# A fused two-block transformer: expert outputs of all passes but the last fetched and weighed by GpSimd during the last pass, the last pass added by TensorE; the even mixer's norm roots in four groups

## The chip, the cores and the metric

The kernel runs on one core of one Trainium2 chip. Times are device microseconds (us) from launch to end. The kernel before takes 3375.63 us, the median of 3 runs (3374.01 to 3377.91). Everything is float32.

## The reference, cut to what matters

256 tokens of width 1024 (and 256 context tokens in the first block) pass two blocks of two layers each. The change touches two places.

Place one, the gated linear attention of layer 0 (4 heads of 128 values, run as two pairs of heads, two directions). Its outputs are normed per token and head, then gated:

```python
def _rms(x, gain, eps=1e-6):
    y = xf * lax.rsqrt(jnp.mean(xf * xf, axis=-1, keepdims=True) + eps)
    return (y * gain.astype(jnp.float32)).astype(x.dtype)
def _gated_readout(o, og, gain):
    return _merge(_rms(o, gain) * jax.nn.silu(og))
```

Place two, the mixture of experts of the very last layer, with the norm and the per-layer input that end the kernel:

```python
def moe_swiglu(x, w_router, w_gate, w_up, w_down):
    top_v, top_i = lax.top_k(logits, TOP_K)             # 2 of 8 experts per token
    top_w = jax.nn.softmax(top_v, axis=-1)
    gates = jnp.sum(jax.nn.one_hot(top_i, N_EXPERTS) * top_w[..., None], axis=-2)
    for e in range(N_EXPERTS):
        out = out + gates[..., e:e + 1] * swiglu(x, w_gate[e], w_up[e], w_down[e])
x = layer_norm(alpha * x + f, ln_ffn_g[i], ln_ffn_b[i])        # alpha * x: "ALPHA X"
x = x + (p[i] @ w_ple_proj[i]) * jax.nn.sigmoid(x @ w_ple_gate[i])
```

## The kernel before, in words

The program is written out by hand, engine by engine, in stages. Between two stages stands `meet()` (L197): each engine drains, raises its semaphore and waits for those of the other three. SyncE issues all weight loads into a ring of three slots (`ring_buf`); it doesn't take part in `meet()`.

**Even mixer, `gla_pairs`.** Sixteen units, eight for each pair of heads (`units`, p = 0 then p = 1), go through a pipeline: TensorE sums and scores, ScalarE exponentials, VectorE masks (L927), GpSimd halves (L894), VectorE adds the levels (`add_levels`, L934), TensorE makes the output (L822, L824), VectorE takes it (`take`, L942). Pair p's token tiles 0 and 1 are complete four units before its end; tile 3 comes with the second last unit and tile 2 with the last. ScalarE squares and sums the outputs (`square`, L859): those of pair 0 while pair 1 runs, all eight of pair 1 after the last unit. GpSimd then takes one root of all 128x16 sums (L904, L906), and VectorE multiplies sixteen 128x128 blocks by root and gate (L970). Then comes a `meet()` and the turning of the result (L256).

**Experts.** `experts` first routes (logits, top two, `place` = the token's rank in its expert, `where` = its row in the DRAM table `moe_rows`, and the number of passes, `total`). A pass handles up to 96 tokens of one expert: 44 MB of weights in twelve items over three slots, an item's load issued when its slot's former item is used up. Seven passes are written out (`FIXED`), the rest run in one hardware loop (L2863) whose count is loaded from `total` by `passes` (L2854); with these inputs the loop runs once, so there are eight passes. In a pass TensorE gathers the tokens of the next one (`gather`, L2919), and the result goes from PSUM through `ye` (ScalarE L3043, VectorE L3083) to `moe_rows` in DRAM (`save`, L2876, in the next pass behind item 2). After the last pass SyncE saves once more, GpSimd fetches each token's two rows with four indirect DMAs (L3103) into the third slot, and VectorE weighs and adds them (L3091, L3093). `clear_rows` (L2647) zeroes the part of `moe_rows` past the first eight passes, much earlier.

**Norm.** `seam_alone` with `LayerNormSeam`: VectorE makes ALPHA X + Y for a token tile (L2436), its statistics (L2439, L2441), GpSimd the root (L2450, L2451), VectorE scales (L2443), TensorE turns (L2483), ScalarE and VectorE write `hT` (L2490, L2498). Behind its roots GpSimd loads the norm's gain and shift (`pool_begin`, L191) and waits for them (L193) before it can reach the `meet()`. `per_layer_input` (L2568, L2576, L2586) ends the kernel; its three weight loads (L223) stand behind the last `save` on SyncE.

## Time and profile before

| what | value |
|---|---|
| median of 3 runs | 3375.63 us |
| profiled execution, its own time | 3372.65 us |
| its span (first to last instruction) | 3370.8 us |
| TensorE busy / VectorE / ScalarE / GpSimd | 3099.1 / 819.7 / 414.5 / 304.9 us |
| granted TensorE clock, mean | 0.96 |
| chain that ended last: TensorE / VectorE / DMA | 81% / 11% / 2% of the span |

1.9 us lie outside the span. All times of the trace count from the span's start. "Idle before" is how long an engine sat before a group of instructions; the arrow names who ended it. The granted clock is 1.00 at 2.4 GHz and 0.50 at 1.2 GHz. TensorE's float32 matmuls appear as two records each, transposes as one.

### The profile page before, as it was taken

The numbers are of one execution on the slowest core, as the hardware profiler recorded it, in microseconds if no ns is written. First come the engines' busy times: TensorE is split into PE (matmuls) and PEld (weight loads), VectorE is DVE, ScalarE is ACT, GpSimd is POOL, SyncE is SP. The second block draws the span as 40 slices with busy tenths as digits, with TensorE's granted clock in tenths as the row PEclk, the third lists the DMA queues.
The fourth block names the chain that finished last, engine by engine and source line by source line (L and its number), as shares of the span: only waits on it lengthen the run. The fifth ranks groups of instructions, "written<-read, shape, count | busy, mean of one in ns | idle before, by whom it ended". The sixth has DMA issues, their size and how long they took to land.

```text
span 3370.8 us, 41515 instructions
## 1 busy us (share of the span) xinstructions
PE 3099.1 (92%) x18118; PEld 1767.8 (52%) x18118; DVE 819.7 (24%) x1556; ACT 414.5 (12%) x1027; POOL 304.9 (9%) x359
## 2 busy tenths in 40 slices
PE   6988779999989999899988999978999999999995
PEld 2456544444447777576656766444434434444442
DVE  1146932000035676500132000253000000000003
ACT  1024121000022212200021000130000000000001
POOL 1123710000002233200000000000000000000000
PEclk9989889999999999999989999978999999999997
DMA  8670001212022122244332343305899999999983
GB/s 345 252 260 1 1 0 63 112 63 106 38 59 63 51 61 60 90 149 167 122 113 113 131 174 138 108 33 204 340 406 359 359 381 388 359 362 407 359 316 117
DMA packets 210612, 609.13 MB, mean 181 GB/s; under 512 B 6076, under 2 KB 55452, under 8 KB 203904
## 3 DMA queue, kind: packets, MB, share of 16 engines
q1 hardware_dynamic: 205024, 592.59, 46.4%
q0 software_dynamic: 4944, 13.28, 1.2%
q8 instruction: 145, 2.38, 0.3%
q10 hardware_dynamic: 464, 0.60, 0.1%
q14 instruction: 35, 0.29, 0.0%
HBM read 600.28 MB, written 6.16 MB: 180 GB/s over the span
## 4 chain that ended last, share of the span: by engine, by line
PE 81%; DVE 11%; issue 3%; ACT 3%; DMA 2%; POOL 1%; POOLq 0%; ACTq 0%; DVEq 0%; PEldq 0%; SPq 0%
PE ps_ffn_gate L606 10%; PE ps_ffn_up L606 10%; PE ps_ffn_down L642 10%; PE ps_moe_down L2971 6%; PE ps_moe_gate L2928 6%; PE ps_moe_up L2928 6%; PE ps_odd L1904 4%; PE ps_lin L1384 3%; PE ps_project L524 3%; PE ps_moe_gate L2933 3%; PE ps_moe_up L2933 3%; PE ps_moe_down L2977 3%; PE ps_lin L296 3%; PE ps_ple_gate L2576 2%; DVE rec_qd L2163 2%
## 5 line engine op out<-in xcount | busy, mean ns | idle before, releaser
L606 PE MATMUL ps_ffn_gate<-hT,ring_buf 128*128 128x256 f32 (+1 forms) x1152 | 341.5, 450 | 4.4 <-issue 2.4
L606 PE MATMUL ps_ffn_up<-hT,ring_buf 128*128 128x256 f32 (+1 forms) x1152 | 336.7, 445 | 1.3
L642 PE MATMUL ps_ffn_down<-ring_buf,ffn_hiddenT 128*128 128x512 f32 x752 | 325.9, 593 | 3.0 <-issue 3.0
L606 PEld LDWEIGHTS ps_ffn_gate<-hT,ring_buf 128*128 128x128 f32 x1152 | 221.1, 193 | 119.3 <-issue 98.1
L606 PEld LDWEIGHTS ps_ffn_up<-hT,ring_buf 128*128 128x128 f32 x1152 | 218.0, 190 | 110.2 <-issue 90.0
L1904 PE MATMUL ps_odd<-ring_buf,hT 128*128 128x256 f32 (+2 forms) x1024 | 237.0, 386 | 8.1 <-ACT hg_kT L2039 6.4
L642 PEld LDWEIGHTS ps_ffn_down<-ring_buf,ffn_hiddenT 128*128 128x128 f32 x752 | 141.8, 190 | 181.9 <-issue 181.9
L691 DVE TENSOR_TENSOR ffn_hiddenT<-ffn_silu_buf,ps_ffn_up 128x256 f32<-128x256 f32 (+1 forms) x72 | 36.2, 502 | 725.4 <-PE ps_ffn_up L606 725.3
L3070 DVE TENSOR_TENSOR moe_hidden_buf<-moe_silu_buf,ps_moe_up 128x768 f32<-128x768 f32 (+1 forms) x32 | 27.3, 854 | 748.4 <-PE ps_moe_up L2933 748.4
L1904 PEld LDWEIGHTS ps_odd<-ring_buf,hT 128*128 128x128 f32 x1024 | 174.4, 193 | 55.4 <-ACT hg_kT L2039 7.9
L2928 PE MATMUL ps_moe_up<-ring_buf,moe_xg_buf 128*64 128x512 f32 (+1 forms) x1024 | 199.5, 542 | 0.0
L2971 PE MATMUL ps_moe_down<-ring_buf,moe_hiddenT 128*64 128x512 f32 x768 | 170.1, 595 | 0.0
L2928 PE MATMUL ps_moe_gate<-moe_third,moe_xg_buf 128*64 128x512 f32 (+1 forms) x768 | 142.8, 524 | 0.0
L663 ACT ACTIVATE ffn_silu_buf<-ps_ffn_gate 128x256 f32<-128x256 f32 (+1 forms) x72 | 32.3, 449 | 840.5 <-PE ps_ffn_gate L606 840.5
L1384 PE MATMUL ps_lin<-ring_buf,hT 128*128 128x448 f32 (+1 forms) x384 | 132.4, 498 | 0.0
L2928 PEld LDWEIGHTS ps_moe_up<-ring_buf,moe_xg_buf 128*64 128x64 f32 x1024 | 70.6, 137 | 111.5 <-issue 103.3
L3019 ACT ACTIVATE moe_silu_buf<-ps_moe_gate 128x768 f32<-128x768 f32 (+1 forms) x32 | 23.4, 730 | 697.1 <-PE ps_moe_gate L2933 697.1
L2971 PEld LDWEIGHTS ps_moe_down<-ring_buf,moe_hiddenT 128*64 128x64 f32 x768 | 53.0, 137 | 103.3 <-issue 102.5
L1384 PEld LDWEIGHTS ps_lin<-ring_buf,hT 128*128 128x128 f32 x384 | 71.6, 192 | 62.6 <-issue 58.2
L2933 PE MATMUL ps_moe_up<-ring_buf,moe_xg_buf 128*32 128x256 f32 (+1 forms) x2048 | 103.5, 354 | 0.0
L2928 PEld LDWEIGHTS ps_moe_gate<-moe_third,moe_xg_buf 128*64 128x64 f32 x768 | 53.0, 137 | 81.9 <-issue 73.8
L3103 POOL DMA_INDIRECT moe_third<-moe_rows,moe_where x4 | 4.0, 988 | 988.0 <-DMA moe_rows<-moe_ye 987.1
(491 smaller groups left out, 3498.0 us busy)
## 6 DMA issues: line engine op xcount, KB each, us to landing
ring_buf<-in_w_exp_up_dram SPq DMA_DIRECT2D x24, 4096.0 KB, 16.3
ring_buf<-in_w_exp_down_dram SPq DMA_DIRECT2D x24, 4096.0 KB, 16.0
moe_third<-in_w_exp_gate_dram SPq DMA_DIRECT2D x16, 4096.0 KB, 17.6
mod_pieces<-in_mod_w_dram SPq DMA_DIRECT2D x40, 1024.0 KB, 6.4
ring_buf<-in_w_exp_gate_dram SPq DMA_DIRECT2D x8, 4096.0 KB, 17.6
ring_buf<-in_odd_w_in_dram SPq DMA_DIRECT2D x40, 512.0 KB, 5.3
moe_third<-in_w_exp_gate_dram SPq DMA_DIRECT2D x8, 2048.0 KB, 10.8
ring_buf<-in_w_exp_up_dram SPq DMA_DIRECT2D x8, 2048.0 KB, 7.8
```

What stands on the lines that cost most here:

```text
L296: mm = nc.tensor.matmul(ps[n % 4][:, 0:hi - lo], hT[:, k, t * P:(t + 1) * P], view[:, k, o:o + hi - lo], start=k == 0, stop=k == parts - 1)
L524: mm = nc.tensor.matmul(ps_y[i % 2][:, h * 512:(h + 1) * 512], of(k, t), view[:, k, :], start=k == 0, stop=k == KD - 1)
L606: mm = nc.tensor.matmul(ps[:, 0:wide], view[:, k, i * P:(i + 1) * P], hT[:, k, first_col:first_col + wide], start=k == 0, stop=k == KD - 1)
L642: mm = nc.tensor.matmul(ps_y[i % 2][:, h, :], hidT[:, b, i * P:(i + 1) * P], view[:, b, h * 512:(h + 1) * 512], start=first, stop=end)
L1384: mm = nc.tensor.matmul(ps_lin[:, n % 4, 0:hi - lo], hT[:, k, t * P:(t + 1) * P], view[:, k, o:o + hi - lo], start=k == 0, stop=k == KD - 1)
L1904: mm = nc.tensor.matmul(ps[:, 0:width], hT[:, k, t * P:(t + 1) * P], view[:, k, 0:width], start=k == 0, stop=k == KD - 1)
L2163: last = nc.vector.tensor_tensor(in_blocks(qd[:, d, l - 1, :], x), in_blocks(qd[:, d, l, :], x), query_factors(d, x), ALU.mult)
L2576: mm = nc.tensor.matmul(ps_gate[i][:, cols], hT[:, k, t * P:(t + 1) * P], view[:, k, :], start=k == 0, stop=k == KD - 1)
L2928: nc.tensor.matmul(ps[j * 64:(j + 1) * 64, 0:half], xg[:, k, 0:WIDE], w[:, k, j * half:(j + 1) * half], start=k == 0, stop=k == KD - 1, ti ...
L2933: mm = nc.tensor.matmul(ps[j * 32:(j + 1) * 32, half:half + quarter], xg[:, k, WIDE:ROOM], w[:, k, j * quarter:(j + 1) * quarter], start=k ...
L2971: nc.tensor.matmul(ps_y[j * 64:(j + 1) * 64, 0:512], x, w[:, b, j * 512:(j + 1) * 512], start=c == 0 and b == 0, stop=c == NP - 1 and b == ...
L2977: mm = nc.tensor.matmul(ps_y[j * 32:(j + 1) * 32, 512:768], x, w[:, b, j * 256:(j + 1) * 256], start=c == 0 and b == 0, stop=c == NP - 1 a ...
```

## The change

**Even mixer.** The squares of pair 1 are taken in three groups: tiles 0 and 1 after unit 11, tile 3 after unit 14, tile 2 after unit 15. GpSimd takes four roots: pair 0 and the first half of pair 1 between the halves of units 14 and 15, the other two after them. VectorE gates in four places: four blocks before the last `add_levels`, eight behind it, two and two after the last `take`.

**Experts.** GpSimd fetches during the last pass: it waits until all passes but the last are saved, fetches the four sets of rows into the ring's third part (free then), makes ALPHA X in `Y`, and adds the rows times `early`, the routing weight where the row comes from an earlier pass and 0 where it comes from the last. The last pass is not saved. Instead VectorE makes `pick_g` (the pick matrix times the gate) at the start of the loop's pass, TensorE turns it (two transposes behind the dummy `gather`), ScalarE copies it to `back`, and after the loop TensorE multiplies it with `ye` (`scatter`: four 96x128 by 96x512 float32 matmuls) into two PSUM tensors, which VectorE adds to `Y` into X. New small operations on VectorE during routing make `gates` (ahead of the table of passes) and `early` (behind it).

**Norm.** X arrives summed, so L2436 falls away; gain and shift are loaded by GpSimd at the start of the experts stage into `Y[:, 0:2]`. `clear_rows` writes one more block. `START` (the first value of each semaphore) is 16, so that the new waits against registers stay positive.

```diff
-START = 4
+START = 16
...
+                square(1, (0, 1), n - 4)
+                square(1, (3,), n - 1)
+                square(1, (2,), n)
...
+                    if u == n - 2:
+                        root(1, 0, 4, slice(0, 2))
+                        root(2, 0, 2, slice(2, 4))
+                root(3, 3, 4, slice(2, 4))
+                root(4, 2, 3, slice(2, 4))
...
+                    if u == n - 1:
+                        gated(0, (0, 1), 1)
                     add_levels(u)
+                gated(0, (2, 3), 1)
+                gated(1, (0, 1), 2)
                 take(n - 1)
...
+                gated(1, (3,), 3)
+                link_v(gated(1, (2,), 4))
...
+            if not self.summed:
+                link_v(nc.vector.scalar_tensor_tensor(out=x, in0=x, scalar=ALPHA, in1=self.made(i), op0=ALU.mult,
+                                                      op1=ALU.add))
...
                 seam.pool_steps(pool)
-                seam.pool_begin(pool)
...
-                                 for p in range(EXPERTS, 13)))
+                                 for p in range(EXPERTS - 1, 13)))
...
+                for i in range(2):
+                    link_v(nc.vector.tensor_scalar(gates[:, i, :, 0], one[:, i, 0, :], w01[:, i, 0:1], None, ALU.mult))
+                    link_v(nc.vector.scalar_tensor_tensor(out=gates[:, i, :, 0], in0=one[:, i, 1, :],
+                                                          scalar=w01[:, i, 1:2], in1=gates[:, i, :, 0],
+                                                          op0=ALU.mult, op1=ALU.add))
+                for h in range(1, PARTS):
+                    last = nc.vector.tensor_copy(gates[:, :, :, h], gates[:, :, :, 0])
...
-                save(n_passes - 1).then_inc(S["moe_all_saved"].handle, 16)
+                sp.wait_ge(S["moe_weighed"].handle, S["moe_weighed"].at(2))
...
+                def scatter(n):
+
+                    pe.wait_ge(S["moe_ye_a"].handle, S["moe_ye_a"].at(0) + n)
+                    pe.wait_ge(S["moe_ye_v"].handle, S["moe_ye_v"].at(0) + n)
+                    pe.wait_ge(S["moe_back"].handle, S["moe_back"].at(0) - FIXED + n)
+                    for i, ps in enumerate((ps_y[:, :], ps_t[:, :, :].rearrange("p k n -> p (k n)"))):
+                        for h in range(2):
+                            mm = nc.tensor.matmul(ps[:, h * 512:(h + 1) * 512], back[:, i, :],
+                                                  ye[:, h * 512:(h + 1) * 512], start=True, stop=True)
+                        mm.then_inc(S["moe_scatter"].handle, 1)
...
+                            if not isinstance(p, int):
+                                turned_back(p)
                         down(p, n0, c)
...
-                for i in range(2):
-                    dve.wait_ge(moe_fetched[2 * i], 16)
...
+                for i, ps in enumerate((ps_y[:, :], ps_t[:, :, :].rearrange("p k n -> p (k n)"))):
+                    dve.wait_ge(S["moe_weighed"].handle, S["moe_weighed"].at(i + 1))
+                    dve.wait_ge(S["moe_scatter"].handle, S["moe_scatter"].at(i + 1))
+                    nc.vector.tensor_tensor(X[:, 2 + i, :], Y[:, 2 + i, :], ps, ALU.add)
...
+                seam.pool_begin(pool)
+                n_passes = passes(pool)
+                pool.wait_ge(S["moe_saved"].handle, S["moe_saved"].at(0) - 16 + n_passes * 16)
+                pool.sem_inc(S["moe_earlier_saved"].handle, 1)
                 pool.wait_ge(S["moe_places"].handle, S["moe_places"].at(1))
...
+                for i in range(2):
+                    link_g(nc.gpsimd.tensor_scalar(Y[:, 2 + i, :], X[:, 2 + i, :], ALPHA, None, ALU.mult))
+                pool.wait_ge(moe_fetched, 64)
+                for i in range(2):
+                    for c in range(2):
+                        row = fetched[:, 2 * i + c, :]
+                        link_g(nc.gpsimd.tensor_scalar(row, row, early[:, i, c:c + 1], None, ALU.mult))
+                        last = nc.gpsimd.tensor_tensor(Y[:, 2 + i, :], Y[:, 2 + i, :], row, ALU.add)
```

VectorE at the end of the even mixer, before (L934 is `add_levels`, L942 `take`, L970 the gating):

```order
L927 TENSOR_TENSOR ring_buf<-ps_pair_scores,pair_mask_table 128x1024 x2
L942 TENSOR_TENSOR even_A<-even_A,ps_pair_out 128x256
L934 TENSOR_REDUCE hT<-ring_buf 128x256
L942 TENSOR_TENSOR even_A<-even_A,ps_pair_out 128x256
L970 SCALAR_TENSOR_TENSOR even_A<-even_A,pair_rstd_buf 128x128 x16
```

and after the change (the same operations are L936, L951, L943, L969):

```order
L936 TENSOR_TENSOR ring_buf<-ps_pair_scores,pair_mask_table 128x1024 x2
L951 TENSOR_TENSOR even_A<-even_A,ps_pair_out 128x256
L969 SCALAR_TENSOR_TENSOR even_A<-even_A,pair_rstd_buf 128x128 x4
L943 TENSOR_REDUCE hT<-ring_buf 128x256
L969 SCALAR_TENSOR_TENSOR even_A<-even_A,pair_rstd_buf 128x128 x8
L951 TENSOR_TENSOR even_A<-even_A,ps_pair_out 128x256
L969 SCALAR_TENSOR_TENSOR even_A<-even_A,pair_rstd_buf 128x128 x4
```

Twelve of the sixteen gatings moved ahead of the last `take`. VectorE from the end of the last pass to the first scaling of the norm, before (L3083 writes `ye`, L2863 ends the loop, L3091 and L3093 weigh):

```order
L3083 COPY moe_ye<-ps_moe_down 32x256 x4
L2863 REGISTER_ALU
L2863 COMPARE_AND_BRANCH
L3091 TENSOR_SCALAR Y<-moe_third,moe_w 128x1024
L3093 SCALAR_TENSOR_TENSOR Y<-moe_third,moe_w,Y 128x1024
L3091 TENSOR_SCALAR Y<-moe_third,moe_w 128x1024
L3093 SCALAR_TENSOR_TENSOR Y<-moe_third,moe_w,Y 128x1024
L210 UNCONDITIONAL_BRANCH
L2529 UNCONDITIONAL_BRANCH
L2436 SCALAR_TENSOR_TENSOR X<-X,Y 128x1024
L2439 BN_STATS ln_stats<-X 128x6 x2
```

and after (L3171 adds the scattered rows):

```order
L3162 COPY moe_ye<-ps_moe_down 32x256 x4
L2905 REGISTER_ALU
L2905 COMPARE_AND_BRANCH
L3171 TENSOR_TENSOR X<-Y,ps_moe_down 128x1024
L3171 TENSOR_TENSOR X<-Y,ps_moe_turn 128x1024
L210 UNCONDITIONAL_BRANCH
L2551 UNCONDITIONAL_BRANCH
L2462 BN_STATS ln_stats<-X 128x6 x2
```

Four weighings and the ALPHA sum gave way to two additions. TensorE behind the loop, after the change (L3021 is the last of the down projection, L3043 `scatter`, L2506 the norm's turning; before, nothing stood between the branch and the turning):

```order
L3021 MATMUL ps_moe_down<-moe_third,moe_hiddenT 32x256 x16
L2905 REGISTER_ALU
L2905 COMPARE_AND_BRANCH
L3038 REGISTER_ALU
L3040 REGISTER_ALU
L3043 MATMUL ps_moe_down<-moe_ye,moe_back_buf 128x512 x2
L3043 MATMUL ps_moe_turn<-moe_ye,moe_back_buf 128x512 x2
L210 UNCONDITIONAL_BRANCH
L2541 UNCONDITIONAL_BRANCH
L2506 MATMUL ps_turned_4<-const,Y 128x128 x16
```

So TensorE's new work stands directly behind its loop branch, with two register operations ahead of it.

## Rows read from the trace of the kernel before

**Rows 1.** Chain of waits, last 80 us: start us, us, what.

```profile
3290.92 1.91 PE ps_moe_down L2977 x32
3294.26 0.44 DVE moe_ye L3083
...
3294.93 3.66 DMA moe_rows<-moe_ye
...
3303.39 9.69 DMA moe_third<-moe_rows,moe_where
...
3314.91 1.24 DVE X L2436
...
3324.05 4.92 DMA ln_shift<-in_ln_ffn_b_dram
...
3329.66 1.11 PE ps_ple_proj L2568 x4
```

**Rows 2.** Timeline of the norm: start us, us, engine, line, operation.

```profile
3316.17 1.29 DVE L2439 BATCH_NORM_STATS2 ln_stats<-X 128x6 f32<-128x512 f32 x2
...
3326.00 1.50 ACT L2490 ACTIVATE hT<-ps_turned,ln_columns 128x128 f32<-128x128 f32 x4 [2.96 <-PE ps_turned L2483]
```

**Rows 3.** Timeline of TensorE in the per-layer input.

```profile
3340.20 7.03 PE L2576 MATMUL ps_ple_gate<-ring_buf,hT 128*128 128x512 f32 x16
```

**Rows 4.** Stretches after the last pass: busy by engine, clock, DMA share, GB/s.

```profile
3293.00:3296.00 3.00, 0.00 (x0) 0.00 (x0) 1.64 (x4) 1.18 (x2) 0.00 (x0) 0.86 0.09 27
3296.00:3330.00 34.00, 4.29 (x18) 3.49 (x19) 13.79 (x22) 3.01 (x8) 6.98 (x10) 0.50 0.71 256
```

**Rows 5.** The loop line's TensorE branch: ns min/median/max, first and last start.

```profile
L2863 PEldq COMPARE_BRANCH  x1: 114/114/114, 3291.4 to 3291.4; - x1
```

**Rows 6.** The drain line of meet(), from 3285 to 3331 us.

```profile
L204 PEldq DRAIN  x2: 13/1008/2002, 3294.8 to 3324.0; - x2
```

**Rows 7.** DMA issued at 3184.23 us: size, us to landing.

```profile
ring_buf<-in_w_exp_up_dram SPq DMA_DIRECT2D x1, 4096.0 KB, 18.1
```

**Rows 8.** Timeline of TensorE: the first use of that item.

```profile
3206.07 7.09 PE L2928 MATMUL ps_moe_up<-ring_buf,moe_xg_buf 128*64 128x512 f32 x32
```

**Rows 9.** DMA queues, 3304 to 3308 us: packets, MB, share of 16 engines.

```profile
q0 software_dynamic: 267, 1.02, 64.2%
q1 hardware_dynamic: 290, 0.59, 39.5%
```

**Rows 10.** Timeline of the end of the even mixer.

```profile
429.40 2.48 POOL L894 TENSOR_TENSOR ring_buf<-ring_buf 128x512 f32<-128x512 f32 x2 [3.92 <-DVE ring_buf L927]
...
431.92 1.89 DVE L934 TENSOR_REDUCE hT<-ring_buf 128x256 f32<-128x1024 f32 x1 [1.14 <-POOL ring_buf L894]
...
435.98 0.42 DVE L942 TENSOR_TENSOR even_A<-even_A,ps_pair_out 128x256 f32<-128x256 f32 x1 [2.17 <-PE ps_pair_out L824]
436.43 0.31 ACT L859 ACTIVATE pair_junk<-even_A 128x128 f32<-128x128 f32 x1 [29.03 <-DVE even_A L942]
...
440.29 2.93 POOL L906 TENSOR_TENSOR pair_rstd_buf<-pair_rstd_buf,const 128x16 f32<-128x16 f32 x1
443.25 4.29 DVE L970 SCALAR_TENSOR_TENSOR even_A<-even_A,pair_rstd_buf 128x128 f32<-128x128 f32 x16 [6.86 <-POOL pair_rstd_buf L906]
448.11 1.57 PEld L256 LDWEIGHTS ps_turn<-const,even_A 128*128 128x128 f32 x8 [12.47 <-issue]
```

**Rows 11.** Groups of GpSimd by form: busy us, mean ns.

```profile
L1489 POOL TENSOR_TENSOR qk_rstd_buf<-qk_rstd_buf,const 128x10 f32<-128x10 f32 x4 | 8.7, 2178 | 0.3
L1839 POOL TENSOR_TENSOR hg_rstd<-hg_rstd,const 128x2 f32<-128x2 f32 x8 | 6.9, 864 | 0.7
```

**Rows 12.** The line of passes(), around 2335 us.

```profile
L2854 PEldq TENSOR_LOAD <-moe_total x1: 491/491/491, 2336.8 to 2336.8; - x1
```

**Rows 13.** The line of gate()'s wait, around 2335 us.

```profile
L2942 PEldq EVENT_SEMAPHORE  x1: 51/51/51, 2338.4 to 2338.4; - x1
```

**Rows 14.** Timeline of VectorE while it routes.

```profile
2327.39 1.03 DVE L2786 TENSOR_SCALAR moe_one<-const,moe_idf 128x8 f32<-128x8 f32 x4
```

More of the change, by code:

```diff
@@ L852, in decays, with square @@
                         .then_inc(S["rec_decays"].handle, 1)
-                def square(p):
-                    act.wait_ge(S["rec_state"].handle, S["rec_state"].at((p + 1) * per))
-                    for t in range(4):
+                def square(p, tiles, taken):
+                    act.wait_ge(S["rec_state"].handle, S["rec_state"].at(taken))
+                    for t in tiles:
                         for e in range(2):
@@ L952, in take, with gated @@
                     last.then_inc(S["rec_state"].handle, 1)
+                def gated(p, tiles, roots):
+                    dve.wait_ge(S["rec_rms"].handle, S["rec_rms"].at(roots))
+                    for t in tiles:
+                        for e in range(2):
+                            h = 2 * p + e
+                            gate = A[:, t, O_G + h * GV:O_G + (h + 1) * GV]
+                            last = nc.vector.scalar_tensor_tensor(out=gate, in0=made(p, t)[:, e, :],
+                                                                  scalar=rstd[:, t, h:h + 1], in1=gate,
+                                                                  op0=ALU.mult, op1=ALU.mult)
+                    return last
                 link_v(nc.vector.memset(state[:, :, :, :], 0.0))
@@ L2388, in program, with __init__ @@
     class LayerNormSeam:
-        def __init__(self, cx, layer, site, tiles, kept, deferred=False):
+        def __init__(self, cx, layer, site, tiles, kept, deferred=False, summed=False,
+                     rows=None):
             self.layer, self.site, self.tiles, self.kept, self.deferred = layer, site, tiles, kept, deferred
-            self.gain = sb(cx, "ln_gain", [P, D])
-            self.shift = sb(cx, "ln_shift", [P, D])
+            self.summed = summed
+            self.gain = sb(cx, "ln_gain", [P, D]) if rows is None else rows[:, 0, :]
+            self.shift = sb(cx, "ln_shift", [P, D]) if rows is None else rows[:, 1, :]
             self.stats = sb(cx, "ln_stats", [P, 2, 2, 6])
@@ L2708, in experts @@
             chosen = sb(cx, "moe_chosen_buf", [P, 2, EXPERTS])
+            gates = sb(cx, "moe_gates", [P, 2, EXPERTS, PARTS])
+            early = sb(cx, "moe_early", [P, 2, 2])
+            limit = sb(cx, "moe_limit", [P, 1])
+            pick_g = sb(cx, "moe_pick_g_buf", [P, 2, ROOM])
+            back = sb(cx, "moe_back_buf", [ROOM, 2, P])
             slot = sb(cx, "moe_slot", [P, 2, 2, EXPERTS])
@@ L3003, in _ @@
                 other_passes(pe, n_passes, one_pass)
+                scatter(n_passes)
             @block.scalar
```

92 lines of the change are left out of this document (55 added, 37 removed).

## The prediction

> **What bounds the kernel now.** I read the page first: TensorE is busy 92% of the span and carries 81% of the chain that ended last. So a change off TensorE pays only where TensorE stands still, and there are two such places in reach. Then I read the chain of waits at the end [rows 1]: the last pass ends at 3292.8 us, and TensorE's next weights-bound work starts at 3329.66. In between stand the copy to `ye`, the save's landing, four fetches (9.69 us from the last issue to landing), weighing, the norm, and last the landing of `ln_shift` (4.92 us), which holds GpSimd and with it the meeting of the engines. The reader is to see that nearly all of it is DMA and VectorE. Third, the timeline at the end of the even mixer [rows 10]: the last output is taken at 435.98, TensorE turns the result at 448.11, and between lie squares, one root of 2.93 us and sixteen gatings of 4.29 us, one behind the other. In the passes themselves TensorE has no idle stretch worth naming, and there the DMAs are close behind it [rows 7, 8].
>
> **Even mixer: -8.1 us.** Before, from the end of `take` (435.98 + 0.42 = 436.40) eight squares and a scaling pass until the root starts at 440.29, 3.86 us; the root takes 2.93 and the gating 4.29, which ends at 447.54; 0.57 us later TensorE starts [rows 10]. After: two squares (an eighth of about 3.45 us each, 0.9), hand-over and scaling 0.4, a root of two sums 0.86 [rows 11], two gatings at 4.29/16 = 0.27 each with their start, 0.6, and the same 0.57. From about 436.5 this gives 439.9 against 448.11, 8.2 us less; I take 8.1. What hides the rest: the roots of eight and of four sums stand on GpSimd ahead of its last halves, where it sat idle 3.92 us [rows 10]. Between 864 ns for two sums and 2178 ns for ten [rows 11] a sum costs 0.164 us, so the two roots cost 1.85 and 1.19, with two scalings 3.7 us in all: it fits by 0.2. Four gatings (1.07 us) fit into VectorE's idle 1.14 before `add_levels`, and eight (2.15) into the 2.17 before the last `take` [rows 10]. All three fits are tight; what they overrun goes on the path in full, since halves, levels and output of the last unit wait there. If scalings on slices cost twice as much and every cover fails a little, 1.5 us come back: bounds -6.5 and -8.6. The next stage finds its weights in the ring, so nothing there takes the gain back.
>
> **End of the passes: -17.1 us.** `ye` is ready at 3294.70 [rows 1] and the norm's first statistics start at 3316.17 [rows 2]: 21.5 us. In its place comes `scatter`. Its earliest start: TensorE's loop branch runs at 3291.4 [rows 5], while its next instruction, the drain, came at 3294.8 [rows 6], with the matmuls over at 3292.8. I read these 3.3 us as the time to get the code behind the loop. It ends just when `ye` is ready, so `scatter` starts at 3294.9. The Trainium skill ("Runtime: NRT & Kernel Launch", Instruction fetch mechanics) says that a branch whose target isn't in the loaded window stalls for a fetch by DMA; by that rule the cost is right, and the trace agrees with 3.3 us on TensorE.
>
> A float32 matmul of 512 columns takes 7.03/8 = 0.88 us at the full clock [rows 3], four take 3.5, and 7.0 at half of it. The granted clock is 0.86 between 3293 and 3296 and 0.50 behind [rows 4]: it fell soon after 3295, when TensorE had stood still for some 2.3 us. With new work from 3294.9 it may stay up, fall at once, or fall and come back; I take the middle, 5.2 us, so the products are there at 3300.1. VectorE's addition of the first tile hides beside the second product, the second costs 1.24 (as L2436, which also reads two tiles [rows 1]), the meeting 0.5: statistics at 3301.9, that is 14.3 us earlier. Ends: 15.9 (full clock) and 12.5 (half throughout). The second L2436 goes as well, on the path of the second tile: 1.2. The last write to `hT` ends at 3326.00 + 1.50 = 3327.5 [rows 2]; with 0.5 for the meeting TensorE could have started at 3328.0 and not at 3329.66 [rows 1], since GpSimd was waiting for `ln_shift`. That load now stands in front: 1.6. Together 14.3 + 1.2 + 1.6 = 17.1. What is late next: the weights of the per-layer input. SyncE issues them now once the slots are free and GpSimd has weighed, so they are no later than before, and before they were issued behind the save. They land in front of TensorE.
>
> GpSimd's new work must end before 3294. Two scalings for ALPHA X, four more, four additions on 128x1024: by L894 (2.48 us for two of 512 columns, rows 10) at most 2.5 us each, 25 us, from about 3197 on, behind the fetches. It ends near 3232, 60 us early.
>
> **What it costs in the passes: +2.1 us.** (a) The fetch moves 4 x 512 KB beside the weights of the last pass. Two queues share: 1.02 MB and 0.59 MB in 4 us, the fetch's queue had 64% [rows 9]; at 0.40 MB/us the 2.1 MB take 5.2 us of all engines. The item issued at 3184.23 lands 18.1 us later, at 3202.3 [rows 7], and TensorE begins on it at 3206.07 [rows 8]: 3.8 us to spare. If the fetch comes wholly ahead of it, it is 1.4 us late, and what follows is delayed no further, since each later item then has that stall in hand. I take +1.4; the ends are 0 and 5.2. The Trainium skill ("DMA: Bandwidth & Descriptors", Queues, rings and completion order) has each engine take turns between its queues packet by packet. That speaks against the change: a fetch of less urgent rows isn't queued behind the weights. The trace agrees, with more than half for the fetch's queue. (b) Two transposes and register operations in the loop: +0.3. (c) Routing: the six operations for `gates` come ahead of the table for which TensorE waits in `passes`. Its load starts at 2336.8 [rows 12] and with the register operations behind it takes some 0.9 us, while `gate` waits until 2338.4 anyway [rows 13]: 0.7 to spare. Four small operations take 1.03 us [rows 14] or less, two copies 0.2: late by 0.4. Ends 0 and 0.6. `early` comes behind the table, the sixth zero block and GpSimd's loads at the front beside other work: nothing, for GpSimd has nothing else to do in the passes, and the first items have many us to spare. `START` is free.
>
> **Sum.** -8.1 - 17.1 + 1.4 + 0.3 + 0.4 = -23.1 us. From the profiled execution's 3372.65 (span 3370.8 and 1.9 around it) that gives 3349.5. The median shown is 3375.63, 3.0 above the profiled one; on it the sum gives 3352.5, which I predict.
>
> **Rivals.**
> 1. The clock holds up during `scatter` and the fetch finds the DMAs free: 15.9 in place of 14.3, no stall. -8.1 - 18.7 + 0.7 = -26.1, 3349.5. For it: TensorE stands still for only 2.1 us. Against: the clock fell after 2.3 us [rows 4], and the queues are full [rows 9].
> 2. The way out costs twice. `scatter` sits between the loop and the next branch, to the meeting. If TensorE must fetch again for that one, 3.3 us come on the path, where before they lay beside the save. The time is worked out from rows 5 and 6; the Trainium skill's rule on branches (same page and section as above) would have it so. With 1.5 us more from the tight covers of the even mixer or the stall: -23.1 + 4.8 = -18.3, 3357.3. For it: the one branch out of this loop did cost this. Against: TensorE reaches the branch while its matmuls still run, so most may hide.
> 3. Slower than before: the fetch starves the weight stream. Place: the items of the last pass behind 3197. Price: all that it delays them beyond 3.8 us. It decides from 3.8 + 24.5 = 28 us of delay; at 33 us the kernel takes 3380. Against: even with 64% of the engines the fetch is through after 5.2/0.64 = 8 us [rows 9], and no row shows rows of 4 KB running so much slower.
> 4. The change doesn't do what it says, because GpSimd is late: it would need 60 us more work than 25. I give it nothing of its own and count it with 3.
>
> **How the numbers follow.** Forecast 0.57, rival 1 0.20, rival 2 0.20, rivals 3 and 4 0.03. A difference under 0.2% (6.7 us) is no change for this measurement. All cases but the last are faster by 18 us or more: faster 0.95, same 0.02 (some of 2 with both ends of its costs), slower 0.03. The forecast's own range is 3349 to 3356 by the bounds of the clock (1.6 and 1.8) and of the stall. For 8 in 10 I go from 3346 (rival 1, even mixer at its best, runs 2 us lower as the three shown differ) to 3361 (rival 2 with 3.7 us more stall).
>
> **What would show it.** Right: TensorE turns the even mixer's result 3.9 us behind `take` in place of 12.1; the products start within 0.3 us of `ye`; the statistics start 7.2 us behind it; no wait on `ln_shift`; one stall of about 1.4 us on a weight item between 3200 and 3220. Wrong: halves of the last unit starting later than GpSimd's neighbours allow, a gap between the branch and the drain behind `scatter`, several stalls on weights, or additions on VectorE waiting for GpSimd.

## The result and the profile after

| | before | after |
|---|---|---|
| median of the runs, us | 3375.76 (3374.01 to 3377.91, 4 runs) | 3354.65 (3353.03 to 3357.11, 4 runs) |
| profiled execution: time, span | 3372.65, 3370.8 | 3353.03, 3351.2 |
| granted clock of TensorE, mean | 0.960 | 0.963 |

The ratio is 0.9935, 95% interval 0.9922 to 0.9947. The change takes 21.1 us off the median, with 18 to 26 by the interval. Forecast were 23.1 us and 3352.5. (The median of before has moved by 0.13 us because a fourth run has joined the three of the first table.)

The timeline of the changed kernel at the end of the passes answers to [rows 1, 2] (start us, length us, engine, line, operation, in brackets the idle time before it and what ended it):

```profile
3292.95 0.86 DVE L3162 COPY moe_ye<-ps_moe_down 32x256 f32<-32x256 f32 x2
3294.05 1.98 PE L3043 MATMUL ps_moe_down<-moe_ye,moe_back_buf 96*128 96x512 f32 x4 [2.13 <-DVE moe_ye L3162]
...
3295.87 1.88 PE L3043 MATMUL ps_moe_turn<-moe_ye,moe_back_buf 96*128 96x512 f32 x4
...
3297.86 1.22 DVE L3171 TENSOR_TENSOR X<-Y,ps_moe_turn 128x1024 f32<-128x1024 f32 x1 [0.49 <-PE ps_moe_turn L3043]
3299.50 1.29 DVE L2462 BATCH_NORM_STATS2 ln_stats<-X 128x6 f32<-128x512 f32 x2 [0.42 <-issue]
...
3309.89 1.12 PE L2590 MATMUL ps_ple_proj<-const,ple_in 128*128 128x128 f32 x4 [1.84 <-ACTq L204]
```

`ye` is complete at 3293.82. The products start 0.23 us later, the statistics 5.7 us later, and TensorE goes on with the per-layer input 16.1 us later; before it was 21.5 and 35.0. No wait on `ln_shift` is left. The stretches of the changed kernel (busy us by engine, clock, DMA share, GB/s) answer to [rows 4]: the clock is whole up to 3299 and then at half for 14 us, where before it was at half for 37.

```profile
3290.00:3299.00 9.00, 5.62 (x42) 2.36 (x40) 4.05 (x6) 1.19 (x2) 0.00 (x0) 1.00 1.05 393
3299.00:3313.00 14.00, 7.05 (x23) 5.06 (x24) 10.19 (x20) 4.89 (x10) 1.50 (x4) 0.52 0.10 40
```

The end of the even mixer after the change answers to [rows 10]:

```profile
430.09 2.49 POOL L896 TENSOR_TENSOR ring_buf<-ring_buf 128x512 f32<-128x512 f32 x2 [0.50 <-DVE ring_buf L936]
431.06 0.41 DVE L951 TENSOR_TENSOR even_A<-even_A,ps_pair_out 128x256 f32<-128x256 f32 x1
431.38 2.15 DVE L969 SCALAR_TENSOR_TENSOR even_A<-even_A,pair_rstd_buf 128x128 f32<-128x128 f32 x4
432.94 0.70 POOL L906 TENSOR_TENSOR pair_rstd_buf<-pair_rstd_buf,const 128x2 f32<-128x2 f32 x1
433.46 1.87 DVE L943 TENSOR_REDUCE hT<-ring_buf 128x256 f32<-128x1024 f32 x1
...
437.50 0.42 DVE L951 TENSOR_TENSOR even_A<-even_A,ps_pair_out 128x256 f32<-128x256 f32 x1
...
439.20 0.70 POOL L906 TENSOR_TENSOR pair_rstd_buf<-pair_rstd_buf,const 128x2 f32<-128x2 f32 x1
439.93 0.61 DVE L969 SCALAR_TENSOR_TENSOR even_A<-even_A,pair_rstd_buf 128x128 f32<-128x128 f32 x2 [1.49 <-POOL pair_rstd_buf L906]
441.12 3.77 PE L256 MATMUL ps_turn<-const,even_A 128*128 128x128 f32 x16 [3.66 <-POOLq L204]
```

TensorE turns the result 3.6 us behind the start of `take`, against 12.1. And the waits of TensorE in the last pass (waited for: us in total, times, longest):

```profile
PE ps_moe_down L3015 <- ACT moe_hiddenT L3089: 1.3, 2, 0.7
PE ps_moe_down L3015 <- DMA ring_buf<-in_w_exp_down_dram: 0.8, 1, 0.8
PE ps_moe_up L2970 <- DMA ring_buf<-in_w_exp_up_dram: 0.2, 1, 0.2
```

**Where the time went.** I cut the execution at seven starts that all the kernels have: the mixer's first L798, the turning L256 behind it, the 21st projection matmul behind that, the odd mixer's first matmul, the first expert matmul, the end of the last `ye`, the first matmul of the per-layer input's projection. Each number is the difference of two such times in one profile. Four rows (e1, e2, e5, e12) are experiments told below.

| us | to mixer | to turning | to 21st proj. | to odd | to expert | to `ye` | to per-layer | to the end |
|---|---|---|---|---|---|---|---|---|
| before | 302.4 | 145.70 | 17.00 | 535.16 | 1338.23 | 956.18 | 34.97 | 41.2 |
| before, further profile (e12) | 302.7 | 147.59 | 18.70 | 536.55 | 1339.48 | 956.18 | 35.03 | 41.3 |
| experts' part alone (e2) | 301.7 | 145.73 | 17.00 | 535.16 | 1338.90 | 959.55 | 16.07 | 41.8 |
| mixer's part alone (e1) | 303.9 | 137.85 | 18.97 | 536.67 | 1339.63 | 956.15 | 35.00 | 41.3 |
| after | 303.1 | 138.05 | 18.72 | 536.57 | 1339.79 | 957.61 | 16.07 | 41.3 |
| after, further profile (e5) | 301.1 | 143.85 | 18.98 | 536.70 | 1340.03 | 957.44 | 16.07 | 41.4 |

Read against the first profile of before, the change won 7.65 in the mixer and 18.9 at the end, paid 1.43 in the passes, and seems to have lost 1.7 + 1.4 + 1.6 in three stretches between mixer and experts, and 0.7 ahead of the mixer: 19.6 us of span in all. These three losses are what the experiments had to explain first. (e2's 959.55 holds a further 1.7 us at half clock: 0.72 was granted between 2337 and 2343, where the changed kernel had 1.00.)

### The profile page after: what moved, and what is told of

Its sections match the earlier page's. It is cut to its first block, busy times and chain, and to the rows that moved or that the text cites. A ratio compares the mean times of both kernels' runs of the same rounds, so it can differ in the third digit from the quotient of the medians.

```text
span 3351.2 us, 41580 instructions
## 1 busy us (share of the span) xinstructions
PE 3108.1 (93%) x18128; PEld 1771.5 (53%) x18128; DVE 819.6 (24%) x1564; ACT 414.9 (12%) x1028; POOL 333.8 (10%) x376
## 4 chain that ended last, share of the span: by engine, by line
PE 80%; DVE 10%; issue 3%; ACT 3%; DMA 2%; another core or an unknown queue 1%; POOL 1%; POOLq 0%; ACTq 0%; DVEq 0%; PEldq 0%
PE ps_ffn_gate L606 10%; PE ps_ffn_up L606 10%; PE ps_ffn_down L642 10%; PE ps_moe_down L3015 6%; PE ps_moe_gate L2970 5%; PE ps_moe_up L2970 5%; PE ps_odd L1924 4%; PE ps_lin L1404 4%; PE ps_project L524 3%; PE ps_moe_down L3021 3%; PE ps_moe_up L2975 3%; PE ps_moe_gate L2975 3%; PE ps_lin L296 3%; PE ps_ple_gate L2598 2%; DVE rec_qd L2183 2%
## 5 line engine op out<-in xcount | busy, mean ns | idle before, releaser
L3147 DVE TENSOR_TENSOR moe_hidden_buf<-moe_silu_buf,ps_moe_up 128x768 f32<-128x768 f32 (+1 forms) x32 | 27.3, 855 | 747.1 <-PE ps_moe_up L2975 726.5
```

## The experiments

My theory after the result (A): two parts of the forecast held or came out better, but a part of the mixer's gain is given back behind it by TensorE's clock. In the changed kernel the clock is at half from 432.3 to 452.8 although TensorE is back at 441.12, so L351 runs at half clock; before it ran at the full one. Rival (B): these stretches fall otherwise in every execution, and the whole gain arrives.

**e1, the mixer's part alone; e2, the experts' part alone.** e1 is the kernel before with the hunks of `square`, `root` and `gated`; e2 is the kernel after without them:

```diff
-                        square(0, range(4), per)
-                square(1, (0, 1), n - 4)
-                square(1, (3,), n - 1)
-                square(1, (2,), n)
+                        square(0)
+                square(1)
```

> The kernel before with the even mixer's four groups alone; the experts' end, the norm rows and the gates as before. Theory A (about 3 us of what the mixer wins is given back behind it, because TensorE restarts 7 to 8 us earlier into a stretch at half clock that ends no earlier, and what is left arrives at the end): the turning L256 starts 7 to 8 us earlier than in the kernel before, the routing 3 to 5 us earlier, and the time is 3371 to 3373, a gain of 3 to 5 us. Rival B (the low stretches fall by chance from run to run, and the whole gain arrives): 3367.5 to 3369, a gain of 7 to 8 us. If the gated half came out at nothing by the clock as well, 3374 or more.

> The change without the even mixer's part: fetches, ALPHA X, weighed rows and adds on GpSimd beside the last pass, norm rows in front, gates early. Theory A: the end of the passes gives 18 to 20 us (19.8 less 1.1 of stall, with the routing's +0.4): 3356 to 3358 us. Rival B (the end gives only what the prediction took, 17.1, less 1.4 and 0.7): 3360 to 3361 us. Between this kernel and the whole change lies what the even mixer is really worth: 2 to 4 us by A, 7 to 8 us by B.

Measured: e1 ratio 0.9976 (0.9966 to 0.9986), that is -8.1 us (-4.7 to -11.5); median 3370.93 against 3379.03 for the kernel before, measured beside it. e2 0.9954 (0.9941 to 0.9967), -15.5 us (-11 to -20). Together 23.6, the whole change's 21.9 (by its ratio) within the intervals: the parts add up. e1's gain is what B said, and e2's lies nearer to B's 15.0 (17.1 less 1.4 and 0.7) than to A's 18; but both intervals still reach A's numbers (5 and 18), and the median of e2, 3362.29, lies above what either had named, as the kernel before was 3.3 us slower beside it than beside the change. L351 took 3.8 us in e1, as A had it, and 2.0 in e2. The times leaned to B and the profiles to A.

**e12, the kernel before once more,** unedited, for a further profile.

> The kernel before, unedited, for a further profile. Theory A expects L351 at 2.0 us and the 21st projection matmul 17.0 us behind the turning, as in the first profile and in that of the experts' part alone; 34.9 to 35.1 us from the last ye to L2568's restart; 535.2 us from the 21st projection matmul to the odd mixer and 1338 to 1339 from there to the first expert matmul, where kernels with an early turning had 536.6 to 536.8 in six of seven and 1339.6 to 1340.1. If these last two differ by chance alone, one of them stands at the later kernels' number here.

Its timeline, time 3379.31 us:

```profile
435.98 1.22 PE L822 MATMUL ps_pair_out<-ring_buf,hT 128*128 128x256 f32 x2 [5.03 <-DVE hT L934]
436.99 1.06 PE L824 MATMUL ps_pair_out<-even_A,hT 128*128 128x128 f32 x4
450.27 3.77 PE L256 MATMUL ps_turn<-const,even_A 128*128 128x128 f32 x16 [12.22 <-POOLq L204]
454.96 2.93 PE L351 MATMUL ps_turned<-mod_lines,const 2*128 2x512 f32 x6 [0.93 <-ACTq L204]
```

The unchanged kernel also shows L351 at half clock (3.78 us for its eight, six in this window), and all three "losses" of the table: 18.70, 536.55, 1339.48. They need no change to appear, and the first profile of before was a lucky one. (Of the third, 1.6 us, e12 shows 1.25; the routing, below, has the rest.) The reverse holds too: e7 and e10 (below), which turn early, have the short times in the last two stretches (535.08 and 1338.85, 535.09 and 1338.41), though e7 then has 959.44 in the passes, as e2. So A falls as an account of the second and third loss: they come with where the stretches at half clock happen to lie.

What stays open is the first one, the 1.7 us behind the turning. L351 took 3.8 us in all eight profiles that have an early turning and idle time before it, and in one of the three with the late turning (before, e2, e12). In ten of these eleven the stretch at half clock around the mixer's end is 20.4 to 20.5 us long (27.3 in e12). In before and e2 it was over 1.0 us ahead of L351, which started 21.4 and 21.5 us behind its beginning; in the eight with the early turning L351 started 12.6 to 13.6 us behind it and so lay inside. So this loss looks like more than chance. The times can't tell: e1's interval of 7 us has room for 1.7. Four pairs of profiles can be made of before and e12 with the changed kernel and e5; their spans differ by 19.6, 15.3, 26.2 and 21.9 us. One pair tells a difference no better than that, and the repeated runs are needed for the rest.

**e3, rows fetched later in the last pass.**

```diff
                 pool.wait_ge(S["moe_saved"].handle, S["moe_saved"].at(0) - 16 + n_passes * 16)
+                pool.wait_ge(S["moe_gate"].handle, S["moe_gate"].at(3) - NP + n_passes * NP)
                 pool.sem_inc(S["moe_earlier_saved"].handle, 1)
```

> The whole change, but GpSimd fetches the rows only when the fourth of the last pass's gate products... is through, some 17 us later, when the weight queues have run ahead of TensorE. Theory: the two waits of the last pass on weights (0.24 and 0.83 us, together 1.07) come from the fetches' bytes beside the weight items and are gone; GpSimd is done with the adds at about 3245 instead of 3229, still 29 us before the two transposes need them. Time 1.0 us under the whole change, 3353 to 3354. Rival: the weight stream is short there whoever else moves bytes (the wait stands in the kernel before as well, elsewhere), then the stall stays and the time is the same; a second rival is that the four fetches only move the wait to a later item, same time.

Measured: ratio 0.9929 (0.9917 to 0.9941), 3353.09 us. TensorE's waits in the last pass were then

```profile
PE ps_moe_down L3015 <- ACT moe_hiddenT L3089: 1.3, 2, 0.7
```

and nothing on a DMA. From the first expert matmul to `ye` it took 956.41 (956.40 in e10, which has the same edit), against 957.61 in the changed kernel and 956.18 before. So the stall is the fetch's doing, worth 1.2 us, and can be had back by waiting. GpSimd started the fetch 55.9 us before `ye` was complete, where it was 103.0 in the changed kernel: 47 us later and not the 17 that I had expected. Its last addition still ended 19.7 us ahead of `ye`. In the time the 1.2 us can't be told from the change's own.

**e4, the norm's rows behind the passes again.**

```diff
                 seam.pool_steps(pool)
+                seam.pool_begin(pool)
...
-                seam.pool_begin(pool)
                 n_passes = passes(pool)
```

> The whole change, but the norm's two rows (ln_gain, ln_shift) are issued by GpSimd behind the passes again, when it enters the norm. Theory: the second tile's ScalarE step waits for ln_shift, as it did in the kernel before at 3316.17 to 3326.00; since the statistics now start 5.7 us behind the rows instead of 12, and GpSimd reaches its issues no earlier than the meeting ahead of the norm, the rows land 6 to 7 us after the issue and the first tile waits too: +2 to +4 us, 3357 to 3359. The prediction's own term for the rows' landing was 1.6 us. Rival: the landing hides behind the statistics and roots of 5 us, under +0.5 us.

Measured: ratio 0.9944 (0.9931 to 0.9957), 3358.59 us, 5.5 above e3 measured beside it. Its timeline:

```profile
3295.08 3.55 PE L3044 MATMUL ps_moe_turn<-moe_ye,moe_back_buf 96*128 96x512 f32 x4
...
3300.38 1.29 DVE L2462 BATCH_NORM_STATS2 ln_stats<-X 128x6 f32<-128x512 f32 x2 [0.43 <-issue]
...
3306.01 1.01 POOL L191 DMA_DIRECT2D Y<-in_ln_ffn_g_dram  x1
3307.02 0.56 POOL L191 DMA_DIRECT2D Y<-in_ln_ffn_b_dram  x1
...
3312.61 1.11 PE L2591 MATMUL ps_ple_proj<-const,ple_in 128*128 128x128 f32 x4 [3.69 <-POOLq L204]
```

TensorE went on 19.62 us behind `ye` in place of 16.07. Two things lie in the 3.55. The second product fell into half clock (3.55 us against 1.88) and put the statistics at 7.39 us instead of 5.69: 1.70, chance again. The rest, 1.85, is TensorE waiting longer for GpSimd (3.69 us against 1.84 for the meeting), which issued the rows only behind its roots. e6 and e9 below, with statistics as late as here (7.38) and the rows in front, went on 17.77 us behind `ye`, 1.85 earlier than e4. That bears out the forecast's 1.6 for the norm rows. My +2 to +4 covers the median but not for its reason: the first tile didn't wait, and the rows alone cost less than 2.

**e5, the change once more,** unedited, beside e6 to e8.

> The whole change once more, unedited, on the chip and in the call of the next three. If the ratio of the first measurement (0.9935) is a property of the kernel, it comes again within 0.0015. If the stretches at half clock fall where they will from execution to execution, the profile shows them elsewhere: theory A says that the one behind the even mixer begins at 431 to 434 and ends at 452 to 456 again, and that L351 takes about 3.8 us in it; rival B says that its place is chance, and L351 then takes 2.0 us as before in about half the profiles.

Measured: 0.9928 (0.9914 to 0.9942), 3353.57 us: the result repeats. Its mixer took 5.8 us longer than in the first profile (143.85 against 138.05) at a mean granted clock of 0.83 against 0.88 over it, while the stretch from `ye` to the per-layer input was the same to 0.01 us. L351 took 3.8 us, where B let me expect 2.0 in half the profiles: this is the part of A that stays open.

**e6 and e9, TensorE kept at work at the mixer's end.** Nothing reads these products. e6:

```diff
+                def keep(count):
+                    for _ in range(count):
+                        nc.tensor.matmul(bank_rest[:, P:512], ident, const[:, P:512], start=True, stop=True)
+                keep(14)
                 output(n - 1)
+                keep(10)
```

> The whole change, and TensorE multiplies const into an unused part of a PSUM bank while it waits at the end of the even mixer: 14 matmuls of 384 columns ahead of the last unit's output, 10 behind it, about 0.32 us each at full clock. Nothing reads them. Theory A (what the mixer won is partly given back because TensorE restarts inside the stretch at half clock): the clock stays at its upper level over the turning L256, L351 and the first matmuls of the projection L524; L351 falls from 3.8 to 2.0 us, the first eight L524 from 5.6 to 3.4, the turning from 3.8 to 3.4: 3.5 to 4.5 us under the unedited change. Rival B (the clock falls there whatever TensorE does, or the time comes back at a later stretch): the same time or, if the 24 matmuls hold back the last unit or the turning, up to 4 us more.

e9 has `keep(8)` and `keep(5)`.

> As the kernel of e6, but 8 matmuls of 384 columns ahead of the last unit's output and 5 behind it. In e6 each ran as two instructions of 0.33 us, so that 14 and 10 of them took 9.2 and 6.6 us and held the output back by 4.0 us and the turning by 2.2 more; these take 5.3 and 3.3 us and fit into the idle 5.5 and 3.7. Theory A: the turning starts as in the unedited change and the first 21 projection matmuls are through 15.9 us behind it (e6) instead of 18.7 to 19.2; before the change it was 17.0: 3 us less in the profile, and 1 to 4 us in the time. Rival B: the clock falls all the same in the 0.2 to 0.5 us that stay idle, and the 18.7 to 19.2 stay.

e6 measured 0.9936 (0.9923 to 0.995), e9 0.9926 (0.9912 to 0.9939), 3352.59 us. The timeline of e9:

```profile
432.91 5.33 PE L844 MATMUL ps_pair_rest<-const 128*128 128x384 f32 x16
438.57 0.70 PE L822 MATMUL ps_pair_out<-ring_buf,hT 128*128 128x256 f32 x2 [0.33 <-DVE hT L949]
439.10 0.61 PE L824 MATMUL ps_pair_out<-even_A,hT 128*128 128x128 f32 x4
439.55 3.39 PE L844 MATMUL ps_pair_rest<-const 128*128 128x384 f32 x10
444.15 1.09 PE L256 MATMUL ps_turn<-const,even_A 128*128 128x128 f32 x8 [1.21 <-POOLq L204]
...
447.56 2.23 PE L351 MATMUL ps_turned<-mod_lines,const 2*128 2x512 f32 x8 [0.93 <-ACTq L204]
```

The clock held over the turning in both; in e6 over L351 too (1.99 us), while in e9 it fell inside L351, for 3.4 us. From the turning to the 21st projection matmul it took 15.67 us (e6 15.86) against 18.6 to 19.2 in the kernels with an early turning and idle there. Locally 3 us are won, as expected. In e6 each matmul became two instructions of 0.33 us, twice what I had reckoned; by the profile they held the last output back by 3.3 us and the turning by 3.2 more, and the median was 3357.01, 3.4 above e5's. In e9 they fit into the idle time, but its time differs from e5's by 1 us in 3353, less than the runs can tell.

**e7, the same around the norm.** `ps_g` and `spare` aren't read.

```diff
                         mm.then_inc(S["moe_scatter"].handle, 1)
+                    nc.tensor.matmul(ps_g[:, 0:512], ident, const[:, 0:512], start=True, stop=True)
...
+                keep(3)
                 for i in range(len(tiles)):
                     seam.pe_turn(pe, i)
+                    keep(2)
```

> The whole change, and TensorE multiplies const into PSUM that nobody reads around the norm behind the passes: 1 matmul of 512 columns behind the scatter, 3 ahead of the first turning, 2 behind each turning. Theory: the 13.7 us at half clock from 3299.5 are gone or shorter; what stands in them of TensorE's on the path is the rest of the two turnings (about 0.4 us) and the head of L2598 (8.2 against 7.0 us in the kernel before): 1.5 to 2.3 us under the unedited change. Rival: the gaps left, up to 2 us, are enough for the clock to fall, then the same time or, by the matmuls in TensorE's way at half clock, up to 1 us more.

Measured: 0.9926 (0.9912 to 0.9939), 3352.11 us. The stretch that stood at 0.52 is now whole:

```profile
3299.00:3313.00 14.00, 11.73 (x42) 5.62 (x41) 10.87 (x20) 4.90 (x10) 1.50 (x4) 1.00 0.17 69
```

From `ye` to the end of the 16th L2598 record it took 23.05 us, against 25.18 to 25.75 in the six kernels whose products also ran at full clock: some 2.2 won (2.1 to 2.7), as expected by its stretch; the time, 1.5 us under e5's, can't tell it.

**e8, four gatings moved from before `add_levels` to the end.**

```diff
-                    if u == n - 1:
-                        gated(0, (0, 1), 1)
                     add_levels(u)
...
                 gated(1, (3,), 3)
+                gated(0, (0, 1), 1)
                 link_v(gated(1, (2,), 4))
```

> The whole change, but the four gatings that stood ahead of the last unit's add_levels (L969 at 431.38, 2.15 us for four, where two later ones take 0.61) stand in VectorE's last idle stretch, the 1.48 us ahead of the last gating. Theory: they were slow because GpSimd's L896 ran beside them, held up add_levels by 1.1 to 2.1 us, and now cost nothing, or 0.6 us at most: add_levels starts 1 us earlier or more and the turning L256 starts 0.9 us earlier. In the time that is 0.9 us less if it all arrives. Rival: VectorE is held by L896 itself at that place (add_levels waits for the halves of GpSimd), so it starts when it did and the four gatings now add up to 1 us at the end.

Measured: 0.9935 (0.9921 to 0.9948), 3355.46 us. Its timeline:

```profile
429.95 0.41 DVE L951 TENSOR_TENSOR even_A<-even_A,ps_pair_out 128x256 f32<-128x256 f32 x1
431.50 1.89 DVE L943 TENSOR_REDUCE hT<-ring_buf 128x256 f32<-128x1024 f32 x1 [1.14 <-POOL ring_buf L896]
...
435.89 1.66 DVE L969 SCALAR_TENSOR_TENSOR even_A<-even_A,pair_rstd_buf 128x128 f32<-128x128 f32 x6
438.15 0.62 DVE L969 SCALAR_TENSOR_TENSOR even_A<-even_A,pair_rstd_buf 128x128 f32<-128x128 f32 x2 [0.60 <-POOL pair_rstd_buf L906]
...
439.35 3.77 PE L256 MATMUL ps_turn<-const,even_A 128*128 128x128 f32 x16 [3.83 <-POOLq L204]
```

`add_levels` (L943) starts 1.55 us behind `take` instead of 2.40, waiting 1.14 for GpSimd as it did before the change. The six later gatings come one every 0.28 us, and the last two wait for GpSimd's root, as in the changed kernel. From the start of the second last `take` to the turning it took 9.4 us, against 10.05 to 10.10 in the seven profiles that have the change's mixer unedited: 0.7 of the 0.9 expected, clear of the scatter of that stretch, and unseen in the time (1.9 above e5's median, within the scatter of the runs).

**e11, the gates behind the table.**

```diff
-                for i in range(2):
-                    link_v(nc.vector.tensor_scalar(gates[:, i, :, 0], one[:, i, 0, :], w01[:, i, 0:1], None, ALU.mult))
...
                 nc.vector.sem_inc(S["moe_table"].handle, 1)
+                for i in range(2):
+                    link_v(nc.vector.tensor_scalar(gates[:, i, :, 0], one[:, i, 0, :], w01[:, i, 0:1], None, ALU.mult))
...
```

> The change with the gates' six instructions on VectorE behind the experts' table instead of ahead of it. Theory: VectorE's chain to the table is 1.2 us shorter, and TensorE's first expert matmul no longer waits for the table: it starts 6.9 to 7.1 us behind the first L2961 instead of 7.4. In the time 0.3 to 0.5 us, which the rounds cannot tell from nothing. Rival: the wait was for the rows copied by ScalarE, and the 7.4 stay.

Measured: 0.9930 (0.9917 to 0.9944), 3353.64 us. The first expert matmul starts 7.04 us behind the first L2961 in place of 7.41 to 7.42 (nine profiles); before the change 6.86 and 7.04. The theory holds: 0.4 us in this stretch.

**e10, all of these together** (e3, e7, e8, e11, `keep(6)` and `keep(5)` in the mixer).

> The change with all that helped by its own stretch of the profile: rows fetched late (e3), TensorE kept at work around the norm (e7) and at the even mixer's end (6 matmuls ahead of the last output and 5 behind it), four gatings last (e8), gates behind the table (e11). If the stretches add up: 1.2 + 2.1 + 3 + 0.8 + 0.3 = 7.4 us under the unedited change, 3346 to 3348. Rival: what is won early meets a later stretch at half clock and up to 3 us of it are given back, 3349 to 3351.

Measured: 0.9912 (0.9897 to 0.9927), 3349.95 us, the lowest of all, 2.2 to 3.7 under e7, e9, e11 and e5; but its interval overlaps theirs, so that it beats the changed kernel isn't shown. I had expected 3346 to 3348; it is the rival's 3349 to 3351 that came. Its timeline shows where a part of the 7.4 is missing:

```profile
443.66 1.09 PE L256 MATMUL ps_turn<-const,even_A 128*128 128x128 f32 x8 [1.65 <-POOLq L204]
...
447.54 3.78 PE L351 MATMUL ps_turned<-mod_lines,const 2*128 2x512 f32 x8 [0.93 <-ACTq L204]
...
3292.27 3.77 PE L3055 MATMUL ps_moe_down<-moe_ye,moe_back_buf 96*128 96x512 f32 x4 [2.13 <-DVE moe_ye L3175]
3295.84 3.46 PE L3055 MATMUL ps_moe_turn<-moe_ye,moe_back_buf 96*128 96x512 f32 x4
```

In this execution the clock fell behind the mixer in spite of the added matmuls, and both products ran at half clock: the statistics started 9.02 us behind `ye`, 3.3 more than in e7.

## Why the prediction was right, step by step

- **Even mixer, -8.1.** Right. To the turning -7.65 in the profile, -8.1 (-4.7 to -11.5) by e1. The whole stage varies by more than that between executions (138.05 and 143.85), but the stretch that was changed doesn't: from the start of the second last `take` to the turning it took 17.74 to 17.78 us in the three profiles with the old mixer and 10.05 to 10.10 in the seven with the new one, 7.7 less. The pieces moved against each other. The tail behind `take` came out 0.3 better. The covers did fail by 0.85, within the 1.5 that the text had allowed: `add_levels` starts 2.40 us behind that `take` (431.06 to 433.46), and 1.55 before the change, by this line of before and the 431.92 of [rows 10]:

```profile
430.37 0.41 DVE L942 TENSOR_TENSOR even_A<-even_A,ps_pair_out 128x256 f32<-128x256 f32 x1
```

  The four gatings between them took 2.15 us instead of 1.07. The line's own view of that stretch, and then that of e8 (operation, count, duration in ns as least/median/most, first and last start):

```profile
L969 DVE SCALAR_TENSOR_TENSOR even_A<-even_A,pair_rstd_buf x4: 339/351/1341, 431.4 to 433.2; 128x128 f32<-128x128 f32 x4
```

```profile
L969 DVE SCALAR_TENSOR_TENSOR even_A<-even_A,pair_rstd_buf x16: 342/344/354, 433.3 to 438.4; 128x128 f32<-128x128 f32 x16
```

  The first of them took 1.34 us while GpSimd's L896 ran to 432.58 beside it (1.34 to 1.36 in all nine profiles with a gating there); in e8, where none stands beside L896, all sixteen take 0.34 to 0.35. The Trainium skill ("SBUF — State Buffer", SBUF: two separate sides) says that a VectorE operation with two SBUF inputs and a GpSimd operation that reads SBUF lock each other out, whichever starts first, for the whole instruction; the traces of the change and of e8 agree for L896. They don't show it for the small roots: beside L906 at 432.94 two gatings took 0.34 and 0.36 us, and the root its 0.70, as long as the one at 439.20 with nothing beside it. GpSimd's roots took 1.67 and 1.01 us where I had taken 1.85 and 1.19, and fitted.
- **End of the passes, -17.1.** The mechanism was right and the term too small: TensorE went on 18.9 us earlier behind `ye`. The mis-sized piece is `scatter`: I took 5.2 us, a middle between full and half clock, and it took 3.7. That is rival 1's clock (its free DMAs didn't come). Over the ten other profiles with `scatter` the statistics stood 5.7 us behind `ye` in six, 7.4 in three and 9.0 in one, 6.5 in the mean, so my 7.2 was no bad price but a little dear. The norm rows were worth 1.85 by e4 (I had 1.6).
- **The code behind the loop.** The row on which I built 3.3 us, TensorE's drain at 3294.8 [rows 6], doesn't carry it: in the changed kernel TensorE was past its branch and at `scatter`'s first instruction 0.2 us later, and then waited for `ye`.

```profile
L2905 PEldq COMPARE_BRANCH  x1: 110/110/110, 3290.6 to 3290.6; - x1
L3038 PEldq ALU_OP  x1: 36/36/36, 3290.7 to 3290.7; - x1
L204 PEldq DRAIN  x1: 3722/3722/3722, 3294.1 to 3294.1; - x1
```

  The last start is the drain behind `scatter`, issued beside its matmuls and over when they are. So the path pays nothing for code, neither on leaving the loop nor at the drain, and rival 2 is out as a price. That no fetch took place isn't shown: one of up to 3.1 us would lie hidden in the wait for `ye` (the next instruction ran at 3293.9). By the Trainium skill's rule on branches ("Runtime: NRT & Kernel Launch", Instruction fetch mechanics) a stall was due only for code outside the loaded window; this trace has no visible one. What fills the 3.3 us in the kernel before stays open: no wait stands there in the program, and the drain came 0.14 us behind the end of `ye` in all three profiles that have it so (before, e12, e1). The start of the products came out right because `ye` was as late as the supposed fetch, which is luck.
- **The fetch, +1.4, and transposes, +0.3.** Measured: two stalls, 0.24 and 0.83, and 1.43 in all from the first expert matmul to `ye`, where 1.7 were forecast. e3 shows that 1.2 of it is the fetch. The size was right, the form was not: I had one stall of 1.4 us and nothing behind it, and the larger of the two (0.83) came on the next item. The queues took nearly equal shares, and not the 64% for the fetch of [rows 9]; this is the changed kernel from 3197 to 3204 us (packets, MB, share of 16 engines):

```profile
q1 hardware_dynamic: 376, 1.47, 52.8%
q0 software_dynamic: 383, 1.37, 49.1%
```

  Rival 3 needed 28 us of delay. The item issued at 3181.93 landed 22.1 us later, 4 more than in [rows 7]:

```profile
ring_buf<-in_w_exp_up_dram SPq DMA_DIRECT2D x1, 4096.0 KB, 22.1
```

  GpSimd's last addition ended at 3229.3, forecast near 3232, with some luck: it began 6 us earlier than the 3197 of the forecast and then waited 6.65 us for the rows, and its scalings took 2.85 us, above my bound of 2.5.
- **Routing, +0.4.** Right: +0.38 to +0.56 in the profiles, and e11 takes 0.4 back.
- **The ranges.** The range of its own, 3349 to 3356, is narrower at its upper end than its terms give: 1.8 for the clock and 3.8 for the stall on 3352.5 make 3358.1. The measured 3354.65 lies inside either. (The squares' 3.86 us are 3.89 from 436.40 to 440.29, which changes nothing.)
- **What the sum left out:** the scatter between executions. The stretches at half clock move between profiles of one kernel, and one of them moved costs or gives 1.3 to 1.9 us. The sum -23.1 stands within the four pairs of profiles (-15.3 to -26.2) and within the interval of the runs (-18 to -26). The four terms as the first pair of profiles has them add up to -7.65 - 18.9 + 1.43 + 0.4 = -24.7; 1.5 of the 1.6 beyond the forecast is the clock in `scatter`, which was good in that profile. That the forecast came within some 2 us of the measured median says no more than that it lies inside this scatter.

## What to carry to other kernels

Before you explain a loss found by comparing two profiles, take the unchanged kernel's profile a second time: here 4.3 us that looked given back (1.70 + 1.39 + 1.25) stood in the unchanged kernel's second profile too. An edit under about 3 us in 3350 is judged by its own stretch in the profile, from one event to the next, with the clock of the stretch beside it. And when work is moved into idle time beside GpSimd, ask which of its operations stand there, not only how long the gap is.

## What the runs showed of the hardware

- A stretch at half clock isn't over when TensorE is back at work: in the changed kernel it ran from 432.3 to 452.8 with TensorE back at 441.12, and L351 took 3.8 us instead of 2.0. Cheap matmuls into unread PSUM kept the clock up at the norm (23.05 against 25.2 us, e7) and in e6, and up to L351 in e9, behind the mixer (15.7 to 15.9 against 18.6 to 19.2), but not in e10, where TensorE stood idle for 0.87 us before the last output and 1.65 before the turning (e9: 0.33 and 1.21).
- VectorE's gating of 128x128 with two SBUF inputs took 1.34 us beside GpSimd's L896 (128x512, 1.27 us) and 0.34 without it; beside GpSimd's root of two sums (0.70 us) it took 0.34 to 0.36.
- An indirect fetch of 2.1 MB beside a full weight queue took half of the DMA engines (49.1%) and delayed TensorE by only 1.1 us (two waits, 0.24 and 0.83); 47 us later (e3) no wait on a DMA was left.
